# Memory values in seven half-size products, and modulation stored between the first units' sums

## The chip, the cores and the metric

The kernel runs on one core of one Trainium2 chip, as one program on its five engines (TensorE, VectorE, ScalarE, GpSimd, SyncE). They run side by side and meet only in semaphores. The metric is the device time of one execution in microseconds; the median over several executions is given.

## The reference, cut to what matters

The model has two blocks, all in float32, on 256 tokens of width 1024. The first block has two layers. Each is a mixer, a cross attention to a memory of 256 rows, and a squared-ReLU MLP. The second block (attention and a delta rule, then 16 experts) takes a modulation vector that depends on `c` alone.

```python
def memory_cross_attention(h, mem, g_mem, w_q, w_kv, w_o):
    mem_n = rmsnorm(mem, g_mem)
    q = (h @ w_q).reshape(b, s, 4, 256)
    k, v = jnp.split(mem_n @ w_kv, 2, axis=-1)         # v: 256 rows x 1024
    p = jax.nn.softmax(jnp.einsum("bqhd,bkhd->bhqk", q, k) * 256 ** -0.5, axis=-1)
    return jnp.einsum("bhqk,bkhd->bqhd", p, v).reshape(b, s, D) @ w_o

def squared_relu_mlp(h, w_up, w_down):                 # 1024 -> 4096 -> 1024
    return jnp.square(jax.nn.relu(h @ w_up)) @ w_down

mod = jax.nn.silu(c) @ w_ada + b_ada                   # 6 * 1024 numbers, second block
```

## The kernel before, in words

**Weights.** They come as units of 1024 x 512 numbers (2 MB) into a ring of six slots. SyncE issues the loads in the order of use; each waits until the unit that was in its slot has been read. TensorE takes the units in order (`take`).

**A column or row product.** `columns` and `rows` (L453, L480) do a unit in full. A float32 matmul stands in the trace as two records, each with a weight load. The memory's values are `rows("xv...")` in `cross` (L779): for each of two halves of the memory's rows, eight matmuls over the 1024 inputs with 512 output columns. A unit is 16 matmuls, 32 records of 128x512. Two units give a layer's values. ScalarE copies them from PSUM to `vt`. They come after the keys (`xk`) and before the queries (`xq`).

**The MLP's second matrix.** Its eight units (i = 0 to 7) are done already as seven products of half size (in `mlp`, L807). A unit is cut in four blocks of 512 x 256, the hidden rows in four of 128 tokens x 512; seven products of sums of blocks replace the eight plain ones. Each product is four matmuls, 8 records of 128x256, so a unit has 56. Products 0 and 1 read the blocks as they are; products 2 to 6 wait for sums (`ws_ready`) that VectorE makes in `prepare` (L1924), nine operations a unit. Two of the sums of hidden rows stand in `hT`, the others' weights in `arena`, `rstd` and the unit itself. Units 0 to 3 accumulate in PSUM banks 0 to 3, units 4 to 7 in banks 4 to 7. When four units are done, ScalarE copies product 0 and VectorE adds up the four output quarters in `collect` (L1962). TensorE then turns them in eight transposes (L849), and VectorE adds the result to the residual, chunk by chunk.

**Modulation.** During the MLP VectorE weighs rows of `w_ada` (`weigh_modulation`, L1857) in six parts a layer. `modulation(i)` (L799) sums a part over partitions: four matmuls with one output column, 8 records, in PSUM bank 4. VectorE's `modulated(i)` (L1873) adds the bias, stores it, and frees the bank. Part 4 is summed after the last `up` unit. Part 5 is summed after `down` unit 0, and TensorE's `fill("ada5", 4)` waits until bank 4 is free of part 4. On VectorE's queue the end of the MLP reads:

```python
prepare(layer, 0)
prepare(layer, 1)
modulated(6 * layer + 4)
modulated(6 * layer + 5)
...
prepare(layer, 2)
```

VectorE runs in order, and `prepare(layer, 1)` waits for products 2 to 6 of unit 0 before it overwrites the sums that they read.

**After the MLP.** The last unit's quarters are collected and turned. The next layer's first projection (`raw_columns`, L473) takes the residual's chunks 0 to 7 in order as each is ready; behind the second layer it is the sum for the final norm.

Of the kernel before, what the change touches and what calls it, by code (L numbers as in the profile page):

```python
# [12 lines left out]
P = 128  # L13
# [147 lines left out]
def program(nc, a, out, plan):  # L161

    ctx = ExitStack()
    with ctx:
# [56 lines left out]
        hsum = [view(hTt, 512 * i, 4, P) for i in range(4)]  # L221
        quarters = [more[:, S * i:S * (i + 1)] for i in range(4)]
# [91 lines left out]
        hs_ready = sem("h_scaled")  # L314
        ws_ready, q_copied, q_ready = sem("weights_and_rows_summed"), sem("first_product_copied"), sem("quarters")
# [48 lines left out]
        WIDE = ("xa0", "xa1")  # L364
        HALF = (slice(0, 4), slice(4, 8))
        TOK = (slice(0, P), slice(P, S))
        FEAT = (slice(0, S), slice(S, 2 * S))
        product_done, down_unit = {}, {}
# [42 lines left out]
        def _(pe):  # L411
# [41 lines left out]
            def columns(tag, rhs, kc=DC, ready=None, middle=None, banks=(None, None)):  # L453

                w, u = take()
                nt = w.shape[2] // P
                for b in range(0, nt, 2):
                    ps = fill(f"{tag}{b // 2}", banks[b // 2])
                    for j in range(2):
                        for k in range(kc):  # L460
                            if ready is not None and b == 0 and j == 0:
                                ready(k)
                            last = mm(ps[:, j * S:(j + 1) * S], w[:, k, (b + j) * P:(b + j + 1) * P],
                                      rhs(k) if callable(rhs) else rhs[:, k, :], k == 0, k == kc - 1)
                    mark(last, f"{tag}{b // 2}", u=u if b + 2 >= nt else None)
                    if b == 0 and middle is not None:
                        norm_of_sum(middle)

            def raw_columns(tag, norm_tag):

                base = 8 * FOLDED.index(norm_tag)
                columns(tag, raw, ready=lambda k: pe.wait_ge(raw_ready, base + k + 1), middle=norm_tag)
# [306 lines left out]
            def cross(layer):  # L779
                columns(f"xk{layer}_0_", raw, ready=lambda k: pe.wait_ge(mn_ready, 9 * layer + k + 1), banks=(5, 6))  # L780
                norm_of_sum(f"xa{layer}")
                columns(f"xk{layer}_1_", raw)
                for i in range(2):
                    w, u = take()
                    rows(f"xv{layer}_{i}_", raw, w, u, 0, 512)
                ready = chunk_wait(h_ready)
                columns(f"xq{layer}_0_", hT, ready=ready)
                columns(f"xq{layer}_1_", hT)
                open_projection(f"xo{layer}_")
                stage = f"xa{layer}"  # L790
                attention(stage, lambda: copied(
                    pe, *(f"x{t}{layer}_{i}_{j}" for t in "qkv" for i in range(2) for j in range(2))),
                    lambda h, part: between_cross(stage, h, part))
# [13 lines left out]
            def mlp(layer):  # L807
# [7 lines left out]
                for i in range(8):  # L815
                    side_, g = divmod(i, 4)
                    if g == 0:
                        pq = [fill(f"pq{layer}_{side_}_{j}", 4 * side_ + j) for j in range(4)]
                    w, u = take()
                    down_unit[layer, i] = u  # L820
                    h = hid[:, 8 * g:8 * g + 8, :]
                    rows_ = {"11": lambda k: h[:, k, TOK[0]], "12": lambda k: h[:, 4 + k, TOK[0]], "22": lambda k: h[:, 4 + k, TOK[1]]}
                    rows_ |= {f"s{j + 1}": lambda k, j=j: hsum[j][:, k, :] for j in range(4)}
                    cols_ = {"11": lambda k: w[:, k, FEAT[0]], "21": lambda k: w[:, 4 + k, FEAT[0]], "22": lambda k: w[:, 4 + k, FEAT[1]],
                             "t1": lambda k: wsum[0][:, k, :], "t2": lambda k: wsum[1][:, k, :], "t3": lambda k: w[:, k, FEAT[1]],
                             "t4": wide_sum}
                    step = 8 * (8 * layer + i)
                    for n, (j, l, r, needs) in enumerate((((0, 0), "11", "11", 0), ((0, 1), "12", "21", 0), ((1, 1), "s1", "t1", 2),
                                                          ((2, 0), "s2", "t2", 4), ((1, 0), "22", "t4", 5), ((2, 1), "s3", "t3", 7),
                                                          ((3, 0), "s4", "22", 8))):  # L830
                        if needs:
                            pe.wait_ge(ws_ready, step + needs)
                        for k in range(4):
                            if side_ == 0 and n < 2 and k % 2 == 0:
                                pe.wait_ge(hid_ready, 16 * layer + 4 * g + 2 * n + k // 2 + 1)
                            last = nc.tensor.matmul(pq[j[0]][:, FEAT[j[1]]], rows_[l](k), cols_[r](k),  # L836
                                                    start=g == 0 and k == 0 and n in (0, 2, 3, 6), stop=g == 3 and k == 3,
                                                    skip_group_check=True)
                        if n >= 2 or (n == 1 and g == 3):
                            mark(last, f"pq{layer}_{side_}_{j[0]}", g == 3, u if n == 6 else None)  # L840
# [59 lines left out]
            mm(sums[1][:, 0:S], ones, raw(7), False, False)  # L900
            mark(mm(sums[1][:, 0:S], epsm, sq[:, 7, :], False, True), "norm_n1")
            mark(mm(sums[0][:, 0:S], ones, sq[:, 7, :], False, True), "norm_final")
# [410 lines left out]
        def _(act):  # L1313
# [155 lines left out]
            def cross(layer, added):  # L1469
# [8 lines left out]
                for i in range(2):  # L1478
                    for t in range(TT):
                        copy(f"xv{layer}_{i}_{t}", vt[:, t, 512 * i:512 * (i + 1)])  # L1480
# [4 lines left out]
            def mlp(layer):  # L1485
# [5 lines left out]
                for i in range(2):  # L1491
                    if i:
                        copied(act, *(f"dn{layer}_0_{f}" for f in range(4)))
                    ps, _ = full(act, f"pq{layer}_{i}_0")
                    fn(quarters[0], ps[:, FEAT[0]], ACT.Copy).then_inc(q_copied, 1)
                    for c in range(4 * i, 4 * i + 4):
# [158 lines left out]
        def _(dve):  # L1655
# [195 lines left out]
            def cross(layer):  # L1851
                sum_pairs(f"xa{layer}")
                norm(f"xa{layer}", lambda c: col(f"xa_norm{layer}", c))
                attention(f"xa{layer}")
                add(f"xo{layer}_", lambda c: col(f"mlp_norm{layer}", c))

# [21 lines left out]
            def mlp(layer, gain=None):  # L1878
                sum_pairs(f"mlp{layer}")
                norm(f"mlp{layer}", lambda c: col(f"mlp_norm{layer}", c))  # L1880
                for n in range(16):
# [27 lines left out]
                for c in range(DC):  # L1909
                    if c == 4:  # L1910
# [5 lines left out]
                    if gain is not None:  # L1916
                        copied(dve, name)
                        V.tensor_scalar(raw(c), xT[:, c, :], gain(c), None, ALU.mult).then_inc(raw_ready, 1)
                        if c > 1:
                            add_square(c - 1)  # L1920
                    elif c > 1:
                        add_both(c - 1)
# [39 lines left out]
            def collect(layer, i):  # L1962
# [12 lines left out]
                V.tensor_tensor(c11, c11, ps[0][:, FEAT[1]], ALU.add).then_inc(q_ready, 1)  # L1975
# [9 lines left out]
            def add_both(c):  # L1985

                dve.wait_ge(norm_sq, 8 * NORMS.index("final") + 2 * c + 2)
                for first_, other in ((sq[:, 0, :], sq[:, c, :]), (raw(0), raw(c))):
                    ins = V.tensor_tensor(first_, first_, other, ALU.add)
                    if c < DC - 2:  # L1990
                        link(ins)
                if c == DC - 2:
                    ins.then_inc(sum_ready, 1)

            def add_square(c):

                dve.wait_ge(norm_sq, 8 * NORMS.index("cd") + c + 1)
                ins = V.tensor_tensor(sq[:, 0, :], sq[:, 0, :], sq[:, c, :], ALU.add)
                if c < DC - 1:
# [375 lines left out]
```

## Time and profile before

| what | before |
|---|---|
| median of 3 runs | 1793.9 us (1791.47 to 1796.63) |
| the profiled execution's own time | 1789.16 us |
| its span in the trace | 1787.4 us, 20576 instructions |
| TensorE matmul busy | 1545.1 us (86%) |
| TensorE weight loads | 1140.7 us (64%), beside the matmuls |
| VectorE | 582.3 us (33%) |
| ScalarE | 260.1 us (15%) |
| GpSimd | 30.2 us (2%) |
| mean granted TensorE clock | 0.936 of full speed |

Starts in the trace count from the first instruction. The profiled execution took 1.8 us more than its span. A row of a timeline merges instructions of one kind that follow each other, and the time in square brackets is what the engine idled before them and for whom. "PEld" is the weight load, which runs beside the matmul.

### The profile page before, as it was taken

The numbers are of one execution on the slowest core, as the hardware profiler recorded it, in microseconds if no ns is written. First come the engines' busy times: TensorE is split into PE (matmuls) and PEld (weight loads), VectorE is DVE, ScalarE is ACT, GpSimd is POOL, SyncE is SP. The second block draws the span as 40 slices with busy tenths as digits, with TensorE's granted clock in tenths as the row PEclk, the third lists the DMA queues.
The fourth block names the chain that finished last, engine by engine and source line by source line (L and its number), as shares of the span: only waits on it lengthen the run. The fifth ranks groups of instructions, "written<-read, shape, count | busy, mean of one in ns | idle before, by whom it ended". The sixth has DMA issues, their size and how long they took to land.

```text
span 1787.4 us, 20576 instructions
## 1 busy us (share of the span) xinstructions
PE 1545.1 (86%) x8896; PEld 1140.7 (64%) x8896; DVE 582.3 (33%) x1259; ACT 260.1 (15%) x610; POOL 30.2 (2%) x52
## 2 busy tenths in 40 slices
PE   6999999999998999999899899989977666655665
PEld 4868688887876777788788788768863222121211
DVE  3633015355633420243556646642330000000000
ACT  1332021000011520210000222222020000000000
POOL 0000000000010000000000002000000000000000
PEclk9999999999999999999999899998979987888877
DMA  9325316664433054157644101432739999999997
GB/s 391 143 94 188 142 48 235 235 253 171 177 141 142 1 192 166 44 210 283 259 147 146 48 1 66 135 107 96 298 126 417 429 429 429 429 429 430 427 429 313
DMA packets 42826, 395.27 MB, mean 221 GB/s; under 512 B 15856, under 2 KB 18288, under 8 KB 19056
## 3 DMA queue, kind: packets, MB, share of 16 engines
q1 hardware_dynamic: 42032, 392.46, 55.4%
q8 instruction: 71, 1.16, 0.3%
q0 software_dynamic: 272, 1.05, 0.2%
q10 hardware_dynamic: 432, 0.44, 0.1%
q14 instruction: 19, 0.16, 0.0%
HBM read 391.31 MB, written 2.62 MB: 220 GB/s over the span
## 4 chain that ended last, share of the span: by engine, by line
PE 72%; DMA 22%; DVE 3%; issue 1%; ACT 1%; ACTq 0%; DVEq 0%
PE pb L445 53%; DMA ring<-in_w_experts 22%; PE pb L836 11%; PE pb L533 6%; DMA small_w<-in_small_w 1%; ACT arena L1315 1%; PE pb L594 1%; PE pb L654 0%; PE pb L1141 0%; DVE arena L1936 0%; DVE hT L1936 0%; DVE rstd L1668 0%; PE pb L1148 0%; PE pb L1001 0%; DVE xT L1915 0%
## 5 line engine op out<-in xcount | busy, mean ns | idle before, releaser
L445 PE MATMUL pb<-hT,ring 128*128 128x256 f32 x2176 | 484.2, 383 | 1.4 <-issue 1.4
L445 PEld LDWEIGHTS pb<-hT,ring 128*128 128x128 f32 x2176 | 413.0, 191 | 64.9 <-issue 9.7
L1315 ACT ACTIVATE arena<-pb 128x512 f32<-128x512 f32 (+4 forms) x166 | 77.9, 480 | 519.5 <-PE pb L445 427.6
L2286 DVE SCALAR_TENSOR_TENSOR side<-side,pb 128x256 f32<-128x256 f32 x16 | 6.7, 421 | 411.6 <-ACT side L1315 411.6
L445 PE MATMUL pb<-ring,hT 128*32 128x512 f32 (+2 forms) x512 | 91.3, 634 | 36.7 <-DMA ring<-in_w_experts 36.7
L533 PE MATMUL pb<-arena,ring 128*128 128x256 f32 x512 | 118.2, 382 | 0.0
L445 PE MATMUL pb<-arena 128*64 128x128 f32 (+5 forms) x592 | 90.4, 420 | 28.5 <-DMA arena<-in_w_experts 16.0
L445 PE MATMUL pb<-ring,arena 128*32 128x512 f32 (+1 forms) x416 | 68.3, 770 | 49.6 <-DMA ring<-in_w_experts 49.6
L533 PEld LDWEIGHTS pb<-arena,ring 128*128 128x128 f32 x512 | 94.9, 190 | 14.6 <-issue 2.9
L445 PEld LDWEIGHTS pb<-arena 128*64 128x64 f32 (+3 forms) x592 | 53.9, 159 | 62.8 <-issue 26.9
L445 PEld LDWEIGHTS pb<-ring,hT 128*32 128x32 f32 (+1 forms) x512 | 32.3, 139 | 84.7 <-DMA ring<-in_w_experts 45.3
L445 PE MATMUL pb<-ring,side 128*32 128x256 f32 x768 | 63.4, 487 | 25.7 <-DMA ring<-in_w_experts 22.8
L445 PEld LDWEIGHTS pb<-ring,arena 128*32 128x32 f32 (+1 forms) x416 | 14.8, 132 | 100.5 <-DMA ring<-in_w_experts 77.1
L1315 ACT ACTIVATE side<-pb 128x256 f32<-128x256 f32 (+2 forms) x44 | 18.5, 421 | 328.3 <-PE pb L445 310.1
L445 PEld LDWEIGHTS pb<-ring,side 128*32 128x32 f32 x768 | 28.0, 133 | 57.5 <-DMA ring<-in_w_experts 30.2
L1867 DVE SCALAR_TENSOR_TENSOR arena<-ring,sml,arena 128x512 f32<-128x512 f32 x84 | 62.9, 749 | 2.0
L836 PE MATMUL pb<-ring,arena 128*128 128x256 f32 x256 | 62.1, 398 | 1.3 <-DVE arena L1889 1.3
L1755 DVE TENSOR_REDUCE sml<-pb 128x2 f32<-128x512 f32 x16 | 11.0, 691 | 149.4 <-PE pb L445 149.3
L1889 DVE TENSOR_SCALAR arena<-pb 128x512 f32<-128x512 f32 x28 | 19.4, 692 | 119.8 <-PE pb L445 119.8
L836 PE MATMUL pb<-arena,hT 128*128 128x256 f32 x256 | 58.3, 381 | 0.0
L445 PE MATMUL pb<-lru_w,ring 128*128 128x256 f32 x224 | 54.8, 389 | 4.0 <-issue 4.0
L836 PE MATMUL pb<-ring,hT 128*128 128x256 f32 x256 | 57.9, 379 | 0.0
(297 smaller groups left out, 1705.8 us busy)
## 6 DMA issues: line engine op xcount, KB each, us to landing
ring<-in_w_dense SPq DMA_DIRECT2D x86, 2048.0 KB, 8.2
ring<-in_w_experts SPq DMA_DIRECT2D x72, 2048.0 KB, 36.3
arena<-in_w_experts SPq DMA_DIRECT2D x24, 2048.0 KB, 35.9
ring<-in_w_dense SPq DMA_DIRECT2D x2, 1536.0 KB, 6.4
cons<-in_cons SPq DMA_DIRECT2D x1, 1808.0 KB, 19.6
xT<-in_xT SPq DMA_DIRECT2D x1, 1024.0 KB, 6.2
side<-in_memT POOLq DMA_DIRECT2D x1, 1024.0 KB, 6.5
out<-xT SPq DMA_DIRECT2D x4, 256.0 KB, 2.2
```

The lines of the kernel that those rows point to most:

```text
L445: return nc.tensor.matmul(o, l, r, start=st, stop=sp)
L533: last = nc.tensor.matmul(proj["banks"][c // 2][:, (c % 2) * S:(c % 2 + 1) * S], w[:, k, (c % 4) * P:(c % 4 + 1) * P], yT[:, k, :], start= ...
L594: last = nc.tensor.transpose(ps[:, c:c + P], pr2[:, n % 4, qb, kb * P:(kb + 1) * P], ident)
L836: last = nc.tensor.matmul(pq[j[0]][:, FEAT[j[1]]], rows_[l](k), cols_[r](k), start=g == 0 and k == 0 and n in (0, 2, 3, 6), stop=g == 3 an ...
L1315: return nc.scalar.activation(o, i, f, **kw)
L1755: V.tensor_reduce(nmx[:, n % 2, :], pairs(ps), AX.X, ALU.max, negate=True).then_inc(mx_ready, 1)
L1867: ins = V.scalar_tensor_tensor(acc, w, csil[:, k:k + 1], acc, ALU.mult, ALU.add)
L1889: V.tensor_scalar(hrelu[:, n % 2, :], ps, 0.0, None, ALU.max).then_inc(free, 1)
L2286: V.scalar_tensor_tensor(tg[:, e % 2, :], tg[:, e % 2, :], 1.0, ps[:, 0:S], ALU.add, ALU.mult).then_inc(eg_ready, 1)
```

## The change

- The four `xv` units are done as seven half-size products each. `prepare_values` makes the sums on VectorE (eight operations for a layer's first unit, four for its second, since the memory's sums serve both); `collect_values` adds the products up into `vt`, seven operations a unit. ScalarE copies only product 0. The first unit uses PSUM banks 0 to 3, the second 4 to 7.
- `modulated(4)` now stands ahead of `prepare(0)`, and `modulated(5)` between `prepare(0)` and `prepare(1)`.
- In the MLP's second matrix product 1 moves from bank 0 to bank 3 (4 to 7 for the second half), and in the units 3 and 7 it comes last, after product 6. `collect`, the transposes and the residual's chunks follow another order (0, 1, 2, 3, 6, 7, 4, 5), as do the readers behind the MLP.

```diff
 def rows / cross, TensorE:
-                    rows(f"xv{layer}_{i}_", raw, w, u, 0, 512)
+                    for n, (j, l, r, sums, weights) in enumerate((((0, 0), "11", "11", 0, 0), ((3, 1), "12", "21", 0, 0),
+                                                                  ((1, 1), "s1", "t1", 1, 1), ((2, 0), "s2", "t2", 2, 2),
+                                                                  ((1, 0), "22", "t4", 0, 3), ((2, 1), "s3", "t3", 3, 4),
+                                                                  ((3, 0), "s4", "22", 4, 0))):
+                        if sums:
+                            pe.wait_ge(vh_ready, 4 * layer + sums)
+                        if weights:
+                            pe.wait_ge(vw_ready, 4 * n_ + weights)
+                        if n < 4:
+                            pv[j[0]] = fill(f"pv{layer}_{i}_{j[0]}", 4 * i + j[0])
+                        for k in range(4):
+                            last = nc.tensor.matmul(pv[j[0]][:, FEAT[j[1]]], rows_[l](k), cols_[r](k),
+                                                    start=k == 0 and n < 4, stop=k == 3, skip_group_check=True)
...
 mlp, TensorE:
+                    order = (0, 2, 3, 4, 5, 6, 1) if g == 3 else range(7)
...
-                        for f in range(4):
+                        for f in (2, 3, 0, 1):
...
-                                pe.wait_ge(q_ready, 8 * layer + 4 * (i == 7) + (1, 2, 4, 3)[2 * (f // 2) + t])
+                                pe.wait_ge(q_ready, 8 * layer + 4 * (i == 7) + (4, 1, 3, 2)[2 * (f // 2) + t])
...
 cross, VectorE:
                 norm(f"xa{layer}", lambda c: col(f"xa_norm{layer}", c))
+                prepare_values(layer, 0)
+                prepare_values(layer, 1)
+                collect_values(layer, 0)
+                collect_values(layer, 1)
                 attention(f"xa{layer}")
...
+            def prepare_values(layer, i):
...
+                used(2)
+                V.tensor_tensor(vw[0], w12, w11, ALU.subtract).then_inc(vw_ready, 1)
+                if i == 0:
+                    V.tensor_tensor(vh[0], h21, h22, ALU.add).then_inc(vh_ready, 1)
+                summed(1)
+                used(3)
+                V.tensor_tensor(vw[1], w22, vw[0], ALU.subtract).then_inc(vw_ready, 1)
...
+                used(4)
+                V.tensor_tensor(vw[2], vw[1], w21, ALU.subtract).then_inc(vw_ready, 1)
...
+                V.tensor_tensor(w12, w22, w12, ALU.subtract).then_inc(vw_ready, 1)
...
 mlp, VectorE:
+                modulated(6 * layer + 4)
                 prepare(layer, 0)
+                modulated(6 * layer + 5)
                 prepare(layer, 1)
-                modulated(6 * layer + 4)
-                modulated(6 * layer + 5)
...
 collect:
                 link(V.tensor_tensor(c12, c11, ps[2][:, FEAT[0]], ALU.add))
-                V.tensor_tensor(c11, c11, ps[0][:, FEAT[1]], ALU.add).then_inc(q_ready, 1)
                 link(V.tensor_tensor(c22, c12, ps[2][:, FEAT[1]], ALU.add))
...
                 V.tensor_tensor(c22, c22, ps[1][:, FEAT[1]], ALU.add).then_inc(q_ready, 1)
-                product(6)
+                product(1)
                 V.tensor_tensor(c12, c12, ps[3][:, FEAT[0]], ALU.add).then_inc(q_ready, 1)
+                V.tensor_tensor(c11, c11, ps[3][:, FEAT[1]], ALU.add).then_inc(q_ready, 1)
```

## Rows read from the trace of the kernel before

**Rows 1.** The page, part 4: the chain that ended last, by engine

```profile
PE 72%; DMA 22%; DVE 3%; issue 1%; ACT 1%; ACTq 0%; DVEq 0%
```

**Rows 2.** Windows by stage: busy us (x records), granted clock, DMA share, GB/s

```profile
core 0: us, PE busy (x) PEld busy (x) DVE busy (x) ACT busy (x) POOL busy (x), PEclk, DMA share, GB/s
...
1180.00:1330.00 150.00, 131.45 (x1128) 112.53 (x1127) 41.38 (x84) 29.62 (x61) 2.94 (x3) 0.88 0.49 183
1330.00:1560.00 230.00, 151.68 (x1362) 61.43 (x1362) 11.96 (x28) 16.82 (x40) 0.00 (x0) 0.87 0.96 407
```

**Rows 3.** The chain in order of time, 1250 to 1400 us: start, us, what

```profile
1330.43 6.44 PE pb L445 x32
...
1358.10 24.81 DMA ring<-in_w_experts
```

**Rows 4.** Timeline of TensorE, value units of layer 0: start, us

```profile
171.49 3.60 PE L445 MATMUL pb<-ring,lru_w 128*128 128x512 f32 x8
...
198.96 6.21 PE L445 MATMUL pb<-hT,ring 128*128 128x256 f32 x28
```

**Rows 5.** Windows: the value units of layers 0 and 1

```profile
171.49:198.96 27.47, 27.47 (x66) 12.16 (x65) 0.00 (x0) 2.39 (x4) 0.00 (x0) 1.00 0.42 153
654.99:682.46 27.47, 27.47 (x66) 12.16 (x65) 0.00 (x0) 2.39 (x4) 0.00 (x0) 1.00 0.42 153
```

**Rows 6.** Timeline of VectorE, its last work ahead of layer 1's values

```profile
645.15 3.26 DVE L1676 SCALAR_TENSOR_TENSOR hT<-xT,cols,rstd 128x256 f32<-128x256 f32 x8
```

**Rows 7.** Timeline of TensorE, layer 0: part 4, down units 0 to 3

```profile
390.10 0.95 PE L445 MATMUL pb<-cons,arena 128*128 128x1 f32 x8
...
395.46 3.86 PE L836 MATMUL pb<-arena,hT 128*128 128x256 f32 x16
...
400.89 3.62 PE L836 MATMUL pb<-ring,hT 128*128 128x256 f32 x16
408.57 1.84 PE L445 MATMUL pb<-cons,arena 128*128 128x1 f32 x8 [4.06 <-DVE sml L1876]
410.27 5.68 PE L836 MATMUL pb<-ring,arena 128*128 128x256 f32 x16
...
424.42 3.62 PE L836 MATMUL pb<-ring,arena 128*128 128x256 f32 x16
...
436.50 3.62 PE L836 MATMUL pb<-ring,arena 128*128 128x256 f32 x16
```

**Rows 8.** Timeline of VectorE, layer 0: sums of down units 0 and 1

```profile
394.72 0.69 DVE L1936 TENSOR_TENSOR hT<-arena 128x512 f32<-128x512 f32 x1
...
400.86 1.22 DVE L1936 TENSOR_TENSOR arena<-ring 128x1024 f32<-128x1024 f32 x1
402.00 0.68 DVE L1936 TENSOR_TENSOR hT<-arena 128x512 f32<-128x512 f32 x1
...
403.92 0.69 DVE L1936 TENSOR_TENSOR hT<-hT,arena 128x512 f32<-128x512 f32 x1
...
408.26 0.15 DVE L1876 TENSOR_TENSOR sml<-pb,cols 128x4 f32<-128x4 f32 x1
```

**Rows 9.** Timeline of TensorE, layer 1: the same place

```profile
885.69 3.62 PE L836 MATMUL pb<-ring,hT 128*128 128x256 f32 x16
893.37 1.84 PE L445 MATMUL pb<-cons,arena 128*128 128x1 f32 x8 [4.06 <-DVE sml L1876]
...
909.17 3.62 PE L836 MATMUL pb<-ring,arena 128*128 128x256 f32 x16
```

**Rows 10.** Windows: part 5's sum in layer 0, and down unit 2

```profile
408.57:410.27 1.70, 1.70 (x9) 1.70 (x9) 0.00 (x0) 0.00 (x0) 0.00 (x0) 0.50 0.96 405
...
424.00:436.00 12.00, 12.00 (x57) 10.58 (x56) 7.24 (x10) 0.00 (x0) 0.00 (x0) 1.00 0.49 176
```

**Rows 11.** Timeline behind layer 1's last down unit, TensorE and VectorE

```profile
981.11 0.42 DVE L1974 TENSOR_TENSOR more<-more,pb 128x256 f32<-128x256 f32 x1 [9.73 <-PE pb L836]
...
982.56 0.27 PE L849 MATMUL pb<-cons,more 128*128 128x128 f32 x1
...
983.84 0.42 DVE L1915 TENSOR_TENSOR xT<-xT,pb 128x256 f32<-128x256 f32 x1
```

More of the change, by code:

```diff
@@ L221, in program @@
         hsum = [view(hTt, 512 * i, 4, P) for i in range(4)]
+        vw = [view(arena, 6144, 4, S), view(arena, 7168, 4, S), view(arena, 10240, 4, S)]
+        vh = [view(arena, 11264 + 512 * i, 4, P) for i in range(3)] + [view(more, 0, 4, P)]
         quarters = [more[:, S * i:S * (i + 1)] for i in range(4)]
@@ L314, in program @@
         hs_ready = sem("h_scaled")
+        vw_ready, vh_ready, vp_ready, v_ready = sem("value_weights_summed"), sem("memory_summed"), sem("value_copied"), sem("values")
         ws_ready, q_copied, q_ready = sem("weights_and_rows_summed"), sem("first_product_copied"), sem("quarters")
@@ L364, in program @@
         WIDE = ("xa0", "xa1")
+        FINISHED = (0, 1, 2, 3, 6, 7, 4, 5)
         HALF = (slice(0, 4), slice(4, 8))
@@ L451, in chunk_wait, with columns @@
                 return lambda k: pe.wait_ge(signal, base + k + 1)
-            def columns(tag, rhs, kc=DC, ready=None, middle=None, banks=(None, None)):
+            def columns(tag, rhs, kc=DC, ready=None, middle=None, banks=(None, None), order=None):
                 w, u = take()
@@ L459, in columns @@
                     for j in range(2):
-                        for k in range(kc):
+                        for i, k in enumerate(order or range(kc)):
                             if ready is not None and b == 0 and j == 0:
-                                ready(k)
+                                ready(i)
                             last = mm(ps[:, j * S:(j + 1) * S], w[:, k, (b + j) * P:(b + j + 1) * P],
-                                      rhs(k) if callable(rhs) else rhs[:, k, :], k == 0, k == kc - 1)
+                                      rhs(k) if callable(rhs) else rhs[:, k, :], i == 0, i == kc - 1)
                     mark(last, f"{tag}{b // 2}", u=u if b + 2 >= nt else None)
@@ L790, in cross, with all_copied @@
                 stage = f"xa{layer}"
-                attention(stage, lambda: copied(
-                    pe, *(f"x{t}{layer}_{i}_{j}" for t in "qkv" for i in range(2) for j in range(2))),
-                    lambda h, part: between_cross(stage, h, part))
+                def all_copied():
+                    pe.wait_ge(v_ready, 8 * (layer + 1))
+                    copied(pe, *(f"x{t}{layer}_{i}_{j}" for t in "qk" for i in range(2) for j in range(2)))
+                attention(stage, all_copied, lambda h, part: between_cross(stage, h, part))
                 project(5)
@@ L827, in mlp @@
                     step = 8 * (8 * layer + i)
[L828 to L830 removed]
+                    products = (((0, 0), "11", "11", 0), ((3, 1), "12", "21", 0), ((1, 1), "s1", "t1", 2),
+                                ((2, 0), "s2", "t2", 4), ((1, 0), "22", "t4", 5), ((2, 1), "s3", "t3", 7), ((3, 0), "s4", "22", 8))
+                    order = (0, 2, 3, 4, 5, 6, 1) if g == 3 else range(7)
+                    for n in order:
+                        j, l, r, needs = products[n]
                         if needs:
@@ L836, in mlp @@
                             last = nc.tensor.matmul(pq[j[0]][:, FEAT[j[1]]], rows_[l](k), cols_[r](k),
-                                                    start=g == 0 and k == 0 and n in (0, 2, 3, 6), stop=g == 3 and k == 3,
+                                                    start=g == 0 and k == 0 and n < 4, stop=g == 3 and k == 3,
                                                     skip_group_check=True)
-                        if n >= 2 or (n == 1 and g == 3):
-                            mark(last, f"pq{layer}_{side_}_{j[0]}", g == 3, u if n == 6 else None)
+                        if n >= 2 or g == 3:
+                            mark(last, f"pq{layer}_{side_}_{j[0]}", g == 3, u if n == order[-1] else None)
                             product_done[layer, i, n] = (pq_bank := fillings[f"pq{layer}_{side_}_{j[0]}"][0], marks[pq_bank])
@@ L1478, in cross @@
                 for i in range(2):
-                    for t in range(TT):
-                        copy(f"xv{layer}_{i}_{t}", vt[:, t, 512 * i:512 * (i + 1)])
+                    b, m = product_done["value", layer, i, 0]
+                    act.wait_ge(filled[b], m)
+                    fn(vt[:, 0, 512 * i:512 * i + S], pb[:, b, 0:S], ACT.Copy).then_inc(vp_ready, 1)
                 for i in range(4):
@@ L1493, in mlp @@
                         copied(act, *(f"dn{layer}_0_{f}" for f in range(4)))
-                    ps, _ = full(act, f"pq{layer}_{i}_0")
+                    b, m = product_done[layer, 4 * i + 3, 0]
+                    act.wait_ge(filled[b], m)
+                    ps = pb[:, b, :]
                     fn(quarters[0], ps[:, FEAT[0]], ACT.Copy).then_inc(q_copied, 1)
-                    for c in range(4 * i, 4 * i + 4):
+                    for c in FINISHED[4 * i:4 * i + 4]:
                         copied(act, f"dn{layer}_{c // 4}_{c % 4}")
@@ L1853, in cross, with used, summed @@
                 norm(f"xa{layer}", lambda c: col(f"xa_norm{layer}", c))
+                prepare_values(layer, 0)
+                prepare_values(layer, 1)
+                collect_values(layer, 0)
+                collect_values(layer, 1)
                 attention(f"xa{layer}")
                 add(f"xo{layer}_", lambda c: col(f"mlp_norm{layer}", c))
+            def prepare_values(layer, i):
+                u, base = value_unit[layer, i], 4 * (2 * layer + i)
+                w = slot_ap(u)
+                w11, w12, w21, w22 = (w[:, HALF[a_], FEAT[b_]] for a_ in range(2) for b_ in range(2))
+                m = [view(t, 0, 4, S) for t in (lru_w_, rtp)]
+                h11, h12, h21, h22 = (m[b_][:, :, TOK[a_]] for a_ in range(2) for b_ in range(2))
+                def used(n):
+                    if i:
+                        b, done = product_done["value", layer, 0, n]
+                        dve.wait_ge(filled[b], done)
+                def summed(j):
+                    dve.wait_ge(vw_ready, base + j)
+                dve.wait_ge(loaded[slot_of[u]], 16 * nth[u])
+                if i == 0:
+                    dve.wait_ge(mn_ready, 9 * layer + 8)
+                used(2)
+                V.tensor_tensor(vw[0], w12, w11, ALU.subtract).then_inc(vw_ready, 1)
+                if i == 0:
+                    V.tensor_tensor(vh[0], h21, h22, ALU.add).then_inc(vh_ready, 1)
+                summed(1)
+                used(3)
+                V.tensor_tensor(vw[1], w22, vw[0], ALU.subtract).then_inc(vw_ready, 1)
+                if i == 0:
+                    dve.wait_ge(vh_ready, 4 * layer + 1)
+                    V.tensor_tensor(vh[1], vh[0], h11, ALU.subtract).then_inc(vh_ready, 1)
+                summed(2)
+                used(4)
+                V.tensor_tensor(vw[2], vw[1], w21, ALU.subtract).then_inc(vw_ready, 1)
+                if i == 0:
+                    V.tensor_tensor(vh[2], h11, h21, ALU.subtract).then_inc(vh_ready, 1)
+                V.tensor_tensor(w12, w22, w12, ALU.subtract).then_inc(vw_ready, 1)
+                if i == 0:
+                    dve.wait_ge(vh_ready, 4 * layer + 2)
+                    V.tensor_tensor(vh[3], h12, vh[1], ALU.subtract).then_inc(vh_ready, 1)
@@ new lines, in collect_values @@
+            def collect_values(layer, i):
+                banks = [fillings[f"pv{layer}_{i}_{j}"][0] for j in range(4)]
+                p = [pb[:, b, :] for b in banks]
+                c11, c12, c21, c22 = (vt[:, t, 512 * i + S * f:512 * i + S * (f + 1)] for t in range(TT) for f in range(2))
+                dve.wait_ge(vp_ready, 2 * layer + i + 1)
+                for n in (4, 5, 6):
+                    b, done = product_done["value", layer, i, n]
+                    dve.wait_ge(filled[b], done)
+                link(V.tensor_tensor(c12, c11, p[2][:, FEAT[0]], ALU.add))
+                V.tensor_tensor(c11, c11, p[3][:, FEAT[1]], ALU.add).then_inc(v_ready, 1)
+                link(V.tensor_tensor(c22, c12, p[2][:, FEAT[1]], ALU.add))
+                link(V.tensor_tensor(c12, c12, p[1][:, FEAT[1]], ALU.add))
+                V.tensor_tensor(c21, c22, p[1][:, FEAT[0]], ALU.subtract).then_inc(v_ready, 1)
+                V.tensor_tensor(c12, c12, p[3][:, FEAT[0]], ALU.add).then_inc(v_ready, 1)
+                dve.wait_ge(v_ready, 4 * (2 * layer + i) + 3)
+                V.tensor_tensor(c22, c22, p[1][:, FEAT[1]], ALU.add).then_inc(v_ready, 1)
+                for j, b in enumerate(banks):
+                    V.memset(spare[:, j:j + 1], 0.0).then_inc(freed[b], 1)
@@ L1908, in mlp @@
                 prepare(layer, 6)
-                for c in range(DC):
-                    if c == 4:
+                for at, c in enumerate(FINISHED):
+                    if at == 4:
                         prepare(layer, 7)
```

46 lines of the change are left out of this document (30 added, 16 removed).

## The prediction

> **What bounds the kernel now.** I read the chain of waits first. TensorE holds 72% of it and DMA 22% [rows 1]. The windows by stage then split the run: from about 1340 us to the end the DMA queues are 96% busy with expert weights, and the granted clock there is low because TensorE waits [rows 2]. The chain in order of time shows what starts that stretch: the routing, a TensorE stage at 1330.43, then the wait for an expert unit at 1358.10 [rows 3]. Expert weights flow into slots that dense work has freed, so the stretch starts later or sooner with the dense part and does not get longer. Hence a microsecond off TensorE's path before 1180 is a microsecond off the total. All that is changed lies there. The timelines of TensorE and VectorE at the three changed places give the rest.
>
> **The values.** A layer's two units take 27.47 us from their first record (171.49) to the first query record (198.96), and the same in layer 1 [rows 4, 5]. TensorE is busy all through, at full clock, and VectorE does nothing [rows 5]. That is 13.73 us a unit. The new form has 56 records of 128x256, as a down unit has now. Down units 2 and 3 start at 424.42 and 436.50, so 12.08 us a unit [rows 7]. Saved: 1.65 us a unit, for four units 6.6 us.
>
> What the seven products ask of VectorE: a wide sum (1024 a lane) has a row of 1.22 us, a memory sum (512) one of 0.68 us [rows 8]. The chain of a down unit's nine sums starts at 400.86 and is done when 0.15 us of modulation starts at 408.26, so 7.4 us [rows 8]. The first value unit has the same sums, with the third wide one in one piece; the second only four wide ones, some 4.8 us. VectorE has them queued behind the norm. In layer 1 that ends at 645.15 + 3.26 = 648.4, and the value unit starts at 655.0 [rows 5, 6]. Its product 2 comes 16 records (3.45 us) later, at 658.4, and needs 1.8 us of sums, ready by about 650.3: 8 us of cover. If the cover were gone, each microsecond would be paid in full. The other sources come no later: the key products read the same memory rows before, and the unit's slot was emptied during the mixer. The two collects of a unit's seven additions (rows of such adds are 0.42 us [rows 11], so about 3 us) lie under unit 2 and under the queries. The first frees bank 3 for the queries: it ends some 3 us into the second unit's 12, so 9 us of cover. ScalarE loses work.
>
> A rule of the Trainium skill speaks against this part, and the trace bears on it. Weight loads cost 10.58 us for 56 records in a stretch where the matmuls fill 12.00 us, so 189 ns each, and they lie beside the matmuls [rows 10]. The Trainium skill ("TensorE: Matmul & The Clock Gate", Part 3: Packing small matmuls) says that a weight load overlaps matmuls in flight only when it targets another row group. All loads here use all rows, so by it the 24 more loads a unit would be exposed. By that rule the sum for this part would be a loss of 11.5 us instead of a gain of 6.6. It is a rival below, with a small chance, since 10.58 and 12.00 do not fit side by side in 12.00 unless they overlap.
>
> **The modulation.** TensorE issues down unit 0's last 16 records at 400.89, so it is through at 404.35. Then it idles 4.06 us until 408.57, released by VectorE's modulation row [rows 7]. VectorE is busy in that gap with the sums of unit 1 and stores part 4 only at 408.26 [rows 8]: it is the bank of part 4 that part 5 waits for. The gap costs more than its length. At 408.57 the granted clock is 0.50, the lower of the two levels [rows 10]. Part 5's eight records take 1.84 us where part 4's took 0.95, and unit 1's first 16 take 5.68 us where unit 2's take 3.62 [rows 7]. That is 0.9 and 2.1 us, so 4.06 + 2.95 = 7.0 us in layer 0.
>
> After the change part 4 is stored before unit 0's sums. Part 4's sum is on TensorE at 390.10, VectorE's first sum starts at about 393.6 (0.69 us row at 394.72, one wide sum earlier) [rows 7, 8], so this adds no wait, only the 0.15 us operation, of which I count 0.1 as the rows overlap. Unit 0 is tight: product 2 starts at 395.46, right after the memory-side sum of 394.72 + 0.69 = 395.41 [rows 7, 8]. So the 0.1 us is paid.
>
> Part 5 then follows unit 0 at once, for 0.9 us. VectorE's `modulated(5)` waits for it, and behind it on VectorE's queue stand all sums of unit 1, which were made early before. This is the new wait. Let TensorE start unit 1 at s. VectorE gets part 5 about 0.2 us after s and starts its sums by s + 0.25. The pair for product 2 is ready 402.68 - 400.86 = 1.8 us later, at s + 2.1, needed at s + 3.45. The pair for product 3 is ready 404.61 - 400.86 = 3.75 us later, at s + 4.0, needed at s + 5.2 [rows 8]. The last is ready at s + 7.6, needed at s + 10.4. The least cover is 1.2 us, so I take no stall. VectorE needs 7.4 us in a unit of 12.08 and is ahead again by unit 2. Were the cover gone, the excess over 1.2 us is paid once a layer.
>
> Layer 0: 404.35 + 0.1 + 0.9 + 12.08 = 417.4 for unit 2's start, against 424.42: 7.0 us. Layer 1: 885.69 + 3.46 = 889.15, plus 13.08 is 902.2, against 909.17: 7.0 us [rows 9]. Together 14.0 us. The next weights are no obstacle: DMA share is 0.96 during part 5 but 0.49 in unit 2 [rows 10], and the slots come free earlier as well.
>
> From rows, the bounds of this part are 4.06 us a layer (the idle alone) and 7.0. Both layers show the same gap and the same long part 5 [rows 7, 9], so I take 7.0. The Trainium skill (same page, Part 1: The HAM clock gate) says that how many matmuls run at the low clock varies between runs of one kernel. By it some executions of before would lack part of the 2.95 us, and the sum would be up to 5.9 us smaller.
>
> **Order in the last units.** Products 0 to 6 cost the same in any order. In units 3 and 7 product 2 now comes 1.73 us earlier, but VectorE has finished that unit's sums by then, since it follows the products of the unit before (it idled 9.73 us ahead of the last collect [rows 11]). At the end, TensorE's first transpose (the end of products) is at T = 982.56. VectorE starts at T - 1.45, does seven additions, and adds the first chunk at T + 1.28, as its own queue allows [rows 11]. After the change five additions are done early. The two that need product 6 and 1 start at about T + 0.28. The first is ready at T + 0.7, two transposes follow (to T + 1.15), and the chunk's add comes at about T + 1.2. Gain 0.1 us a layer. The bounds are a gain of 0.4 us (VectorE free at T + 1.0, if the transposes hid) and a loss of 0.4. The four chunks behind are VectorE's either way.
>
> **Sum.** 6.6 + 14.0 + 0.2 = 20.8 us. Profiled, 1789.16 becomes 1768.4. That execution lies 4.7 us under the median 1793.9, and the terms do not depend on which is taken: 1793.9 - 20.8 = 1773.1.
>
> **Rivals.**
> 1. The slow stretch after the gap is not saved: TensorE's lower clock appears elsewhere behind the next short idle, or is absent from the unprofiled runs. 20.8 - 5.9 = 14.9 us, so 1779.0. For it: after any idle of some microseconds the same fall could come. Against: both layers agree. Chance 9%.
> 2. The values gain nothing, because sums or a bank come 8 to 9 us late twice. 14.2 us, 1779.7. Against: VectorE has nothing in 27.47 us [rows 5]. 5%.
> 3. Weight loads are exposed in the new units: 24 x 189 ns = 4.5 us a unit more, 1.65 less, four times: +11.5. With the rest, -14.2 + 11.5 = -2.7, so 1791.2. Against: rows 10, as above. 2%.
> 4. The change doesn't do what it says for the total, because the expert stretch is paced by its 2 MB loads from the start of the run, not from the routing. Then the gain is waited away and 1793.9 stays. For it: DMA share 0.96 there. Against: before it the share is 0.49 [rows 2], and the stretch begins behind TensorE's stage [rows 3]. 6%.
> 5. The other side: VectorE's sums and TensorE's products read and write the same buffers at once in the value units, and slow TensorE's records. It decides where the loss in 224 records passes 20.8 us, at 93 ns a record, so 309 ns instead of 216. At 330 ns: 224 x 114 ns = 25.5 us lost, 1798.6. Against: at 400.89, with VectorE busy with sums, 16 records take 3.62 us as they do elsewhere [rows 7, 8]. 3%.
>
> **How the numbers follow.** My forecast, 1773, has 75%, with its own range of 1768 to 1779: half the spread of the runs before (2.6 us) either way, and a new stall of 1 to 2 us in unit 1 or in the values. The range 1766 to 1781 takes in rivals 1 and 2 and leaves out 3, 4 and 5 (11%). A change of 0.3% (5.4 us) is about what a measurement of this kernel tells from none: faster is 75 + 9 + 5 = 89%, same 2 + 6 = 8%, slower 3%.
>
> **What the profile of the changed kernel would show.** Values: 56 records of 128x256 a unit in place of 32 of 128x512, 24.2 us for a layer's two, without a VectorE wait. Modulation: TensorE's idle for VectorE's modulation row gone, part 5 in about 0.95 us behind unit 0, clock 1.0 there, and unit 1's product 2 without a wait. Collect: the first chunk's add about 1.2 us after the last product. Expert stretch: as long as before, starting 21 us earlier. The prediction is wrong if TensorE waits for `vw_ready`, `vh_ready` or unit 1's sums, if a low clock shows up at another place, or if the expert stretch grows.

## The result and the profile after

| | before | after |
|---|---|---|
| median, first set | 1794.76 us (4 runs) | 1772.13 us (1769.93 to 1775.36, 4 runs) |
| ratio | | 0.9877, 95% interval 0.9863 to 0.9890 |
| the profiled execution | 1789.16 us | 1769.93 us |
| its span | 1787.4 us | 1768.1 us |

After is 1.2% faster, 22.6 us by medians and 19.2 us between the two profiled executions. 20.8 us less was forecast, so 1773.1.

The chain of waits of after, by engine (answers to [rows 1]):

```profile
PE 74%; DMA 23%; DVE 2%; issue 1%; ACT 1%; ACTq 0%; DVEq 0%
```

Windows of after at its four places: the value units of both layers, part 5 of the modulation with down unit 1 behind it, and the projection that follows layer 0's MLP. Columns as in [rows 2]:

```profile
173.51:197.68 24.17, 24.17 (x113) 21.28 (x112) 7.61 (x15) 1.37 (x3) 0.00 (x0) 1.00 0.49 174
651.48:675.65 24.17, 24.17 (x114) 21.28 (x112) 7.97 (x16) 1.36 (x3) 0.00 (x0) 1.00 0.49 174
402.57:403.40 0.83, 0.83 (x10) 0.83 (x8) 0.00 (x0) 0.00 (x0) 0.00 (x0) 1.00 0.83 355
403.38:415.55 12.17, 12.17 (x59) 10.72 (x58) 11.58 (x15) 0.00 (x0) 0.00 (x0) 1.00 0.48 176
493.00:498.20 5.20, 5.17 (x16) 4.31 (x17) 2.19 (x6) 0.80 (x2) 0.00 (x0) 0.67 0.56 239
```

The value units take 24.17 us where [rows 5] have 27.47, with TensorE busy in all of it. Part 5 and unit 1 run at full clock, where [rows 10] have 0.50. The last line has no row before the prediction: a stretch at clock 0.67, so partly at the lower level and partly at the higher, where before ran at the higher level throughout.

Timeline of TensorE in after, layer 0, the place of [rows 7]:

```profile
388.61 0.95 PE L449 MATMUL pb<-cons,arena 128*128 128x1 f32 x8
...
399.12 3.62 PE L869 MATMUL pb<-ring,hT 128*128 128x256 f32 x16
402.57 0.95 PE L449 MATMUL pb<-cons,arena 128*128 128x1 f32 x8
403.38 3.70 PE L869 MATMUL pb<-ring,arena 128*128 128x256 f32 x16
406.92 3.62 PE L869 MATMUL pb<-arena,hT 128*128 128x256 f32 x16
...
415.55 3.62 PE L869 MATMUL pb<-ring,arena 128*128 128x256 f32 x16
```

Timeline of VectorE in after, the place of [rows 8]:

```profile
403.55 0.16 DVE L1975 TENSOR_TENSOR sml<-pb,cols 128x4 f32<-128x4 f32 x1 [4.39 <-PE pb L449]
403.63 1.22 DVE L2035 TENSOR_TENSOR arena<-ring 128x1024 f32<-128x1024 f32 x1
404.78 0.68 DVE L2035 TENSOR_TENSOR hT<-arena 128x512 f32<-128x512 f32 x1
```

Part 5 follows the 16 records that start at 399.12 with no gap. VectorE now idles 4.39 us for part 5, starts unit 1's sums 0.25 us after unit 1 does, and has the first pair at 405.46. TensorE takes it at 406.92: a cover of 1.4 us, and no wait.

Timeline of TensorE in after behind layer 0's last down unit. Product 1, the last, starts at 487.22 and is issued by 488.95. The transposes read the first finished quarter at 489.71; the next projection starts at 493.03:

```profile
487.22 1.89 PE L869 MATMUL pb<-ring,arena 128*128 128x256 f32 x8
...
489.71 1.06 PE L882 MATMUL pb<-cons,more 128*128 128x128 f32 x8 [0.60 <-DVE more L2079]
493.03 2.50 PE L449 MATMUL pb<-lru_w,ring 128*128 128x256 f32 x8 [2.25 <-issue]
495.32 3.08 PE L449 MATMUL pb<-root_pairs,ring 128*128 128x256 f32 x8
498.24 1.89 PE L449 MATMUL pb<-lru_w,ring 128*128 128x256 f32 x8
```

The same place of before. Here the projection follows the transposes at once:

```profile
499.28 0.63 PE L849 MATMUL pb<-cons,more 128*128 128x128 f32 x4 [0.20 <-DVE more L1981]
499.75 1.89 PE L445 MATMUL pb<-lru_w,ring 128*128 128x256 f32 x8
501.48 1.52 PE L445 MATMUL pb<-root_pairs,ring 128*128 128x256 f32 x6
503.47 0.70 PE L445 MATMUL pb<-root_pairs,ring 128*128 128x256 f32 x2 [0.48 <-DVE root_pairs L1918]
504.01 1.89 PE L445 MATMUL pb<-lru_w,ring 128*128 128x256 f32 x8
```

From the last product's end to the projection's second column group it was 504.01 - 497.81 = 6.2 us, and is 498.24 - 488.95 = 9.3 us. So the change's third part costs 3.1 us in layer 0 of this execution. The releaser in the brackets, "issue", names nothing. TensorE's program there calls `fill("cd_qc0")`, which waits for PSUM bank 0, and bank 0 now holds a chunk that VectorE adds third (at 492.51), not first.

The 3.1 us are two prices, and a second execution of the same kernel (after_copy below) separates them. Its last product is issued by 492.48, and it has the same wait, but no low clock behind it:

```profile
496.57 1.97 PE L449 MATMUL pb<-lru_w,ring 128*128 128x256 f32 x8 [2.26 <-issue]
498.37 1.89 PE L449 MATMUL pb<-root_pairs,ring 128*128 128x256 f32 x8
500.10 1.89 PE L449 MATMUL pb<-lru_w,ring 128*128 128x256 f32 x8
```

There the distance is 500.10 - 492.48 = 7.6 us: the wait alone costs 1.4 us more than before, and the lower clock behind it, where it comes, 1.7 more.

### The profile page after: what moved, and what is told of

It is laid out like the page before. It is cut to its first block, busy times and chain, and to the rows that moved or that the text cites. A ratio compares the mean times of both kernels' runs of the same rounds, so it can differ in the third digit from the quotient of the medians.

```text
span 1768.1 us, 20858 instructions
## 1 busy us (share of the span) xinstructions
PE 1539.0 (87%) x8992; PEld 1158.1 (66%) x8992; DVE 617.0 (35%) x1327; ACT 257.1 (15%) x606; POOL 30.3 (2%) x52
## 4 chain that ended last, share of the span: by engine, by line
PE 74%; DMA 23%; DVE 2%; issue 1%; ACT 1%; ACTq 0%; DVEq 0%
PE pb L449 51%; DMA ring<-in_w_experts 22%; PE pb L869 11%; PE pb L538 6%; PE pb L810 3%; DMA small_w<-in_small_w 1%; PE pb L599 1%; PE pb L659 0%; ACT arena L1348 0%; PE pb L1174 0%; DVE rstd L1704 0%; PE pb L1181 0%; PE pb L882 0%; PE pb L1034 0%; DVE xT L2399 0%
## 5 line engine op out<-in xcount | busy, mean ns | idle before, releaser
L449 PE MATMUL pb<-arena 128*64 128x128 f32 (+5 forms) x592 | 95.0, 445 | 28.0 <-DMA arena<-in_w_experts 15.9
L869 PE MATMUL pb<-ring,arena 128*128 128x256 f32 x256 | 58.5, 380 | 0.8 <-DVE arena L1988 0.8
L449 PE MATMUL pb<-root_pairs,ring 128*128 128x256 f32 (+1 forms) x288 | 55.5, 342 | 0.5 <-issue 0.5
```

Of the source, the lines that this page charges most:

```text
L449: return nc.tensor.matmul(o, l, r, start=st, stop=sp)
```

## The experiments

Each was timed against before on the same chip. "Places" are distances between TensorE starts in its profiled execution: the values (end of the keys to the first query), part 4 to part 5 of the modulation (P4-P5), part 5 to the first rotation behind layer 0's MLP, or to the first record of the second block behind layer 1's.

| kernel | ratio (95%) | median | values 0, 1 | P4-P5 0, 1 | P5 to rotation | P5 to block 2 |
|---|---|---|---|---|---|---|
| before | | 1796.35 | 27.47, 27.47 | 18.47, 18.12 | 120.04 | 103.56 |
| after | 0.9877 (0.9863, 0.9890) | 1772.13 | 24.17, 24.17 | 13.96, 13.96 | 120.28 | 100.68 |
| mod_only | 0.9906 (0.9893, 0.9920) | 1779.70 | as before | 14.31, 13.96 | 117.18 | 100.75 |
| values_only | 0.9937 (0.9925, 0.9950) | 1784.88 | 24.2, 24.2 | 18.12, 18.12 | 120.32 | 103.42 |
| order_only | 1.0011 (1.0002, 1.0020) | 1797.87 | as before | 18.47, 18.12 | 122.96 | 103.56 |
| banks_in_turn | 0.9868 (0.9855, 0.9882) | 1773.05 | 24.2, 24.2 | 13.96, 13.96 | 117.13 | 100.69 |
| filled_gap | 0.9931 (0.9918, 0.9943) | 1784.61 | as before | 18.47, 18.12 | 117.25 | 100.82 |
| part5_late | 0.9856 (0.9841, 0.9871) | 1770.42 | 24.2, 24.2 | 13.95, 13.96 | 117.14 | 100.68 |
| no_order | 0.9862 (0.9849, 0.9876) | 1771.46 | 24.2, 24.2 | 13.96, 13.97 | 117.19 | 100.74 |
| before_copy | 0.9997 (0.9986, 1.0008) | 1795.95 | 27.47, 27.47 | 18.47, 18.12 | 120.12 | 103.59 |
| after_copy | 0.9872 (0.9853, 0.9892) | 1773.46 | 24.2, 24.2 | 13.96, 13.96 | 118.60 | 100.69 |

The kernels were timed in four sets, and each ratio is against the before of its own set. The medians of before in the later sets were 1796.35, 1796.64 and 1796.49; after's row belongs to the first, with 1794.76.

**mod_only.** The two stores of modulation moved, nothing else:

```diff
+                modulated(6 * layer + 4)
                 prepare(layer, 0)
+                modulated(6 * layer + 5)
                 prepare(layer, 1)
-                modulated(6 * layer + 4)
-                modulated(6 * layer + 5)
```

> Before, with only the two stores of modulation moved (part 4 ahead of unit 0's sums, part 5 between the sums of units 0 and 1). Theory: the idle of 4.06 us and the half clock behind it both go, 7.0 us a layer, so about 14.0 us less than before; TensorE never waits for unit 1's sums. Rival: only the idle goes and a low clock turns up elsewhere, 8.1 us less. Second rival: the stores' new wait holds unit 1's sums back, and less than 8 us is gained.

By places: 18.47 - 14.31 + 120.04 - 117.18 = 7.0 us in layer 0, 18.12 - 13.96 + 103.56 - 100.75 = 7.0 us in layer 1. 14.0 us, as the theory says; the rival of 8.1 is out. The medians say 16.7, which is 2.7 more (below).

**values_only.** The seven products with their sums and collects, on the kernel before.

> Before, with only the memory's values in seven half-size products a unit. Theory: 24.2 us in place of 27.5 for a layer's two units, 6.6 us less than before in all, with no wait of TensorE for a sum. Rival: the 24 more weight loads a unit are exposed (189 ns each), 11.5 us more than before. Rival: sums or banks are late and nothing is gained, within 1 us of before.

3.3 us a layer in the units. Both rivals are out: 112 weight loads lie beside the records in 24.17 us, and TensorE waits for no sum. The medians say 11.5, where the places of this kernel show 7.3 in all (below).

**order_only.** Product 1's bank and place, and the order of transposes and chunks, on the kernel before.

> Before, with only the order changed: product 1 in bank 3 and last in units 3 and 7, transposes and chunks in the order 0 1 2 3 6 7 4 5. Theory from the trace of after: the next projection's bank 0 now takes the third chunk instead of the first, so TensorE starts it some 2.4 us later and part of it at the lower clock; about 3 us more than before, all at the end of layer 0's MLP, and nothing at the end of layer 1's. The prediction on record says 0.2 us less. Rival: the 3 us in the trace of after are the clock's and not the bank's; then this kernel starts the projection late too but loses under 1 us.

The place shows 122.96 against 120.04, 2.9 us lost, and nothing at layer 1's (103.56). The whole is 1.5 us slower by medians, or 2.0 by the ratio, whose interval is 0.4 to 3.6. The order alone is a loss. Here too part of the projection ran at the lower clock (its first 16 records took 5.2 us, not 3.5), so the 2.9 us are the bank's wait with the clock behind it.

**banks_in_turn.** After, with the transposes in banks 0, 1, 2, 3 in the order in which they are made:

```diff
-                        for f in (2, 3, 0, 1):
-                            ps = fill(f"dn{layer}_{i // 4 - (i == 5)}_{f}", f)
+                        for at_, f in enumerate((2, 3, 0, 1)):
+                            ps = fill(f"dn{layer}_{i // 4 - (i == 5)}_{f}", at_)
```

> After, with the transposes written to banks 0 to 3 in the order in which they are made, so that the first chunk added frees bank 0. If bank 0 is the cause: the projection behind layer 0's MLP starts about 1.3 us after the first chunk's transposes as in before, its second column group starts 6.2 us after the last product instead of 9.3, and the total is 3 us under after, 1769. If it is not: no change of that stretch.

Its timeline behind layer 0's last down unit (the last product is issued by 494.89):

```profile
493.16 1.89 PE L869 MATMUL pb<-ring,arena 128*128 128x256 f32 x8
495.66 1.07 PE L882 MATMUL pb<-cons,more 128*128 128x128 f32 x8 [0.60 <-DVE more L2079]
496.63 1.97 PE L449 MATMUL pb<-lru_w,ring 128*128 128x256 f32 x8
498.43 1.60 PE L449 MATMUL pb<-root_pairs,ring 128*128 128x256 f32 x6
500.50 0.70 PE L449 MATMUL pb<-root_pairs,ring 128*128 128x256 f32 x2 [0.48 <-DVE root_pairs L2017]
501.04 1.89 PE L449 MATMUL pb<-lru_w,ring 128*128 128x256 f32 x8
```

The wait is gone, and 501.04 - 494.89 = 6.2 us again. That settles bank 0 as the cause of the wait. The expected total of 1769 did not come: 1773.05 is not told from after's time, since the intervals overlap. So the gain is shown at the place and not in the whole time.

**filled_gap.** Before, with work on constants in the gap:

```diff
                     if i == 0:
+                        for _n in range(9):
+                            mm(pb[:, 5, 0:S], ident, con("m_dil", 2, S)[:, 0, :], True, True)
                         modulation(6 * layer + 5)
```

> Before, with nine matmuls on constants (18 records of 128x256, 3.9 us, into a bank that is free then) between down unit 0 and part 5 of the modulation. TensorE still waits for bank 4, but is busy nearly all of the gap. Their result is not used. If the lower clock comes from the idle: part 5 in about 0.95 us and unit 1's first 16 records in 3.6, so 2.9 us a layer and 5.9 us less than before although work was added. If the clock falls for another reason: the time stays that of before.

Timeline of TensorE in it, layer 0, the place of [rows 7]:

```profile
411.96 4.05 PE L445 MATMUL pb<-cons 128*128 128x256 f32 x18
416.19 1.02 PE L445 MATMUL pb<-cons,arena 128*128 128x1 f32 x8 [0.18 <-DVE sml L1878]
417.07 3.70 PE L836 MATMUL pb<-ring,arena 128*128 128x256 f32 x16
```

The bank wait stands (P4-P5 is 18.47 and 18.12, as in before), but the clock stays up. Part 5 takes 1.02 us and unit 1's first 16 records 3.70, against 1.84 and 5.68. That gives back 2.8 us a layer, with 36 records of work more. So the gap had two prices, and the second hangs on the idle alone. In the whole time this kernel gained more than the 5.6 us of its places: 12.0 us by medians, where 5.9 were expected. Nothing at the two places accounts for the other 6.4 (below).

**part5_late** and **no_order.** The first is banks_in_turn with part 5 stored behind both units' sums; the second is the change without its third part.

> The kernel with the banks in turn, with part 5 stored behind both units' sums (part 4 still ahead of them). Unit 1's sums are then made during unit 0 as in before. If storing part 4 early is all that counts: the same time as with the banks in turn, within 1 us. If the wait that part 5's store puts ahead of unit 1's sums costs something: up to 2 us less.

> Before, with the values and the modulation changed and the order as it was: the change without its third part. Theory: 6.6 + 14.0 = 20.6 us less than before, and 3 us less than after, since the wait for bank 0 behind layer 0's MLP isn't there. If the order were worth 0.2 us as predicted, it is 0.2 us slower than after.

In part5_late the places are those of banks_in_turn within 0.1 us, and the two ratios are not told apart. Storing part 4 early is all of the modulation's gain; where part 5 is stored costs nothing, because of the cover. no_order has 117.19 where after has 120.28, 3.1 us less. The 3 us expected in the whole time did not come: its median is 0.7 us under after's, which the intervals do not tell from nothing.

**part5_late_old_order.** no_order, with part 5 stored behind both units' sums.

> Before with the values in seven products and part 4 stored ahead of unit 0's sums, part 5 behind both units' sums, the order as before. If part 4's early store is all of the gain: the same places in the trace as the change without its order, 21 to 25 us less than before, and 3 us under after.

Ratio 0.9872 (0.9853 to 0.9891), median 1773.26 us, places as in no_order. The 3 us under after that were expected did not come: after's copy had the same ratio in the same set. In its trace the bank's wait cost 1.4 us, not 3.1.

**before_copy** and **after_copy.** The two kernels unchanged.

> Before itself, unchanged, timed as if it were another kernel, to see what a comparison of equal kernels gives. The parts timed alone gained 3 to 7 us more than their places in the trace show (16.9 where the trace says 14.4, 11.3 where it says 7.0, 12.4 where it says 5.6). If that is chance between sets of runs: a ratio within 0.2% of 1 here, not 0. If the unprofiled runs of before lose time that its profile doesn't show: 1.000, and the excess is real.

> After itself, unchanged, once more, in one call with the others. By the places in the trace 18.5 us less than before (7.0 values, 14.4 modulation, 3.1 lost to the bank), by the first measurement 22.6.

before_copy gave 0.9997 (0.9986 to 1.0008), so two equal kernels come out equal. after_copy gave 0.9872 (0.9853 to 0.9892), median 1773.46. The gain of 22 to 23 us is real, and the places show 18 in after and 20 in its copy. One thing that differs between executions, whatever the kernel, is the start, the chain's wait for the first small load. It has two lengths. This line is of before's profiled execution:

```profile
1.75 10.47 DMA small_w<-in_small_w
```

And this is of banks_in_turn's:

```profile
1.85 15.85 DMA small_w<-in_small_w
```

In the thirteen traces it is short six times and long seven times, in old and new forms alike. Before and its copy were profiled with the short one, and these executions lie 5.6 and 6.2 us under their medians; the copy's is the fastest of its 12. After was too, and lies 2.2 us under its own. But after's copy had the long one and still lies 2.6 us under its median, so the first load is not the whole of it.

**sums_late.** After, with the cover of the value sums taken away:

```diff
                 if i == 0:
                     dve.wait_ge(mn_ready, 9 * layer + 8)
+                    b, done = product_done["value", layer, 0, 1]
+                    dve.wait_ge(filled[b], done)
```

> After, with VectorE made to wait for the first value unit's product 1 before it makes that unit's sums, so that the cover is gone. Theory: the first pair comes 0.3 + 1.8 us after product 1, so TensorE waits 2.1 us once a layer and the value units take 26.3 us in place of 24.2. Rival: the wait grows over the later sums as well, 4 us or more, since VectorE needs 7.4 us for a unit's sums.

Windows of it: the wait and the first 16 records behind it, in layer 0 and in layer 1:

```profile
175.04:177.22 2.18, 0.16 (x1) 0.00 (x1) 1.88 (x3) 0.00 (x0) 0.00 (x0) 1.00 0.95 406
177.22:180.79 3.57, 3.57 (x17) 3.06 (x17) 3.57 (x5) 0.00 (x0) 0.00 (x0) 1.00 0.39 165
657.00:659.18 2.18, 0.16 (x2) 0.00 (x1) 1.89 (x3) 0.00 (x0) 0.00 (x0) 1.00 1.00 428
659.18:664.42 5.24, 5.24 (x16) 4.32 (x17) 5.24 (x7) 0.00 (x0) 0.00 (x0) 0.67 0.25 106
```

TensorE waits 2.02 us once in each layer, as expected; the later sums keep ahead. But the units take 2.3 us more in layer 0 and 4.0 us more in layer 1: behind the second wait the clock was 0.67 and the same 16 records took 5.24 us, not 3.57. The one execution took 1778.93 us; it is a single one, so only its places are used here.

## Why the prediction was right, and where it was not

- **The values: right.** 3.30 us a layer forecast, 3.30 measured. VectorE's first collect freed its bank at 188.8, long before the queries at 197.7. Another 0.7 us went from the queries to the MLP and ahead of down unit 0, which I had not forecast and do not explain.
- **The rule on weight loads: the trace decides against it.** The Trainium skill ("TensorE: Matmul & The Clock Gate", Part 3: Packing small matmuls) lets a weight load overlap matmuls in flight only when it targets another row group. Here 112 loads of 190 ns, all on the same rows, 21.28 us together, lie beside 24.17 us of records in a row, as 10.58 lay beside 12.00 before [rows 10]. The 11.5 us that the rule would have cost are not there.
- **The modulation: right in size and mechanism.** 14.0 us forecast, 14.0 by mod_only's places. The forecast timetable of unit 1 (sums start at s + 0.25, pair at s + 2.1) came true to 0.1 us. filled_gap shows the split: 4.1 us of idle and 2.8 us of clock a layer.
- **The rule that the low clock varies between runs: not at the gap, but elsewhere.** The Trainium skill (same page, Part 1: The HAM clock gate) says that the number of matmuls at the low clock varies between runs of one kernel. At the gap of 4.06 us it was there every time, in all four traces that have the gap (before, its copy, order_only, values_only). At shorter waits the trace agrees with the rule: behind the bank's wait the clock was 0.67 in after and 1.00 in its copy. Rival 1's time did not come. But the prediction's sign of being wrong, a low clock at another place, did show: behind the bank's wait, and in the mixer of layer 1, where the profiled after had a granted clock of 0.53 from 568.98 to 579.79 (below). mod_only's places show that the modulation's 14.0 us are not less for it.
- **The order: wrong.** The failed step is "The four chunks behind are VectorE's either way", with a gain of 0.1 us a layer. In layer 1 it came (first chunk added 1.21 us after the last product, before 1.28). In layer 0 it was a loss of 3.1 us in after and of 1.4 us in its copy. I followed the data from quarter to chunk and not the PSUM banks. The banks kept their numbers when the order turned, so the next stage's first bank came free third and not first; in after, part of the projection then ran at the lower clock as well.
- **The expert stretch: it moved and did not grow.** From the expert stage's first product (1330.43, now 1313.50) to the end it was 457.0 us and is 454.6 us. Rival 4 is out. The prediction's remark that the clock is low there because TensorE waits is not to be read from [rows 2], which have 0.87 there and 0.88 in the stretch ahead of it.
- **The sum.** By places: 6.6 + 0.7 + 14.0 - 3.1 = 18.2. The profiled pair differs by 19.2, with other low-clock stretches in each. The medians differ by 22.6, and the parts alone also gained more by medians than at their places (16.7 for 14.0, 11.5 for 7.3). filled_gap has 12.0 for 5.6, and order_only loses 1.5 by medians and 2.9 at its place. Every kernel so comes out 1 to 6 us better against before than its places say, also order_only and values_only, which still have before's gap. That points at before's own unprofiled executions, which are slower than its two traces by some 6 us, and not at the changes; the cause is not shown. The first load's two lengths may have fallen unevenly, or these executions met the low clock more often. Some 4 us so stay open. The forecast of 20.8 was some 3 us too high for the order and lacked these 4, and 0.7 us elsewhere. These errors point opposite ways: that it came within 2 us of the measured 22.6 is in part luck.

## What to carry to other kernels

When an order of production is turned, follow the buffers as well as the data: list who takes each bank next, and give out the banks in the new order. Price an idle of TensorE with what comes behind it: here 4.1 us of waiting cost 7, each time, and 2.25 us of waiting were followed by the lower clock in one execution and not in another. Compare two traces of one kernel before a difference of 2 us is put down to a change. An engine in order that frees a resource late because of work ahead of it is cured by moving the small freeing operation, not by speeding the work up.

## What the runs showed that I had not expected

- A wait of 2.02 us was followed by full clock in one layer and by 0.67 in the other, in one execution (sums_late). The 2.25 us idle in after was followed by 0.67 as well, and the same idle in its copy by 1.00.
- The stretch from the first rotation behind layer 0's MLP to layer 1's keys took 98.3 us in before and 100.6 in mod_only, with the same instructions: the first attention heads behind a 1.9 us wait ran at the higher clock in one (eight records in 0.93 us) and at the lower in the other (1.53 us). Such a stretch is worth 2.3 us, either way. It is no property of the kernel: with the same wait, after had these eight records in 1.29 us and its copy in 0.93.
- The first load of the run took about 10.5 or about 15.7 us, and the value units of layer 0 start some 5 us later with the long one (171.5 to 174.2 us, against 176.5 to 179.5).
